# One core, Trainium2: w_in blocks reordered, the SSD groups and GLA heads laid beside the weight stream at fixed pieces

## The reference

```
proj = h @ w_in                      # 256 x 20,560 columns; z, xbc, dt, q, k, v, g, gk, two gates
xbc  = silu(conv4(xbc) + b)          # 4096 columns x, then 1024 B, 1024 C
# SSD: 64 heads in 8 groups, chunks of 128 tokens
seg  = a_cs[i] - a_cs[j];  decay = exp(where(i >= j, seg, -inf))
y    = (C B^T * decay) (x dt) + exp(a_cs) C state_before + D x
y    = grouped_rms_norm(y * silu(z))
# GLA: 4 heads, chunks of 64 tokens
gk   = log_sigmoid(gk_lr @ W + b) / 16;  G = cumsum(gk) in a chunk
o    = tril((q/16 e^G)(k e^-G)^T) v + (q/16 e^G) S
S    = e^{G_last} S + (k e^{G_last - G})^T v
o    = rms_norm(o) * silu(g)
merged = sigmoid(gate_s) * (y @ w_ssd_branch) + sigmoid(gate_g) * (o @ w_gla_branch)
return merged @ w_out
```

## Time and profile before

| what | value |
|---|---|
| time, median of 3 runs | 3322.92 us (3320.24 to 3323.34) |
| time of the profiled execution | 3322.72 us |
| its span | 3321.2 us |
| TensorE matmul busy | 3054.7 us, 92% |
| VectorE busy | 1859.4 us, 56% |
| ScalarE busy | 1442.5 us, 43% |
| GpSimd busy | 57.8 us, 2% |
| mean granted clock of TensorE | 0.957 |

### The profile page before, as it was taken

The page is one execution under the profiler, slowest core; times in us unless marked ns, Lnnn a source line. Parts: engine busy times, 40 slices in busy tenths (PEclk is TensorE's granted clock), DMA queues, the critical chain, the costliest instruction groups (busy, mean ns, idle before and its releaser), DMA issues.

```text
span 3321.2 us, 35212 instructions
## 1 busy us (share of the span) xinstructions
PE 3054.7 (92%) x13922; PEld 2496.4 (75%) x13922; DVE 1859.4 (56%) x2379; ACT 1442.5 (43%) x1865; POOL 57.8 (2%) x37
## 2 busy tenths in 40 slices
PE   9999999899889999799899999999788898888898
PEld 7888887777768666578688888887677677777676
DVE  4444446777675555555555645555545646545645
ACT  4444445444544444444443434434434445434444
POOL 0000000100110000000000000000000000000000
PEclk8999999999999999899999999999899999899899
DMA  6777775555557455476466565655566566666564
GB/s 213 218 220 218 217 227 170 165 184 188 173 168 262 139 184 166 149 265 213 159 194 178 199 190 180 204 174 178 181 191 194 173 201 195 196 198 191 177 188 159
DMA packets 348474, 634.25 MB, mean 191 GB/s; under 512 B 37328, under 2 KB 60180, under 8 KB 345236
## 3 DMA queue, kind: packets, MB, share of 16 engines
q1 hardware_dynamic: 268736, 506.13, 49.6%
q10 hardware_dynamic: 79572, 125.85, 11.2%
HBM read 578.47 MB, written 53.43 MB: 190 GB/s over the span
## 4 chain that ended last, share of the span: by engine, by line
PE 73%; DVE 12%; DMA 6%; ACT 5%; ACTq 2%; issue 2%; DVEq 0%
PE bank L873 21%; PE bank L875 21%; PE bank L874 21%; DVE w_lo L1482 4%; DVE arena L1569 2%; ACT w_hi L903 2%; PE bank L479 2%; DMA arena<-in_sin 1%; PE bank L726 1%; PE bank L745 1%; PE bank L547 1%; ACTq L1346 1%; PE bank L638 1%; PE bank L645 1%; ACT arena L982 1%
## 5 line engine op out<-in xcount | busy, mean ns | idle before, releaser
L1482 DVE TENSOR_TENSOR w_lo<-raw,w_hi 128x1024 fp32r<-128x1024 f32 (+2 forms) x980 | 1174.5, 1217 | 1051.9 <-ACT w_hi L903 1044.0
L873 PE MATMUL bank<-w_lo,x_hi 128*128 128x512 f32 (+1 forms) x3920 | 1555.6, 397 | 28.3 <-DVE stage L1987 19.1
L874 PE MATMUL bank<-w_hi,x_hi 128*128 128x512 f32 (+1 forms) x3920 | 1533.3, 391 | 0.0
L875 PE MATMUL bank<-w_hi,x_lo 128*128 128x512 f32 (+1 forms) x3920 | 1533.2, 391 | 0.0
L903 ACT ACTIVATE w_hi<-raw 128x1024 fp32r<-128x1024 f32 (+2 forms) x980 | 999.0, 1044 | 1097.0 <-PE bank L875 582.5
L873 PEld LDWEIGHTS bank<-w_lo,x_hi 128*128 128x128 f32 x3920 | 750.4, 191 | 194.1 <-DVE stage L1987 20.3
L875 PEld LDWEIGHTS bank<-w_hi,x_lo 128*128 128x128 f32 x3920 | 748.5, 191 | 154.6
L874 PEld LDWEIGHTS bank<-w_hi,x_hi 128*128 128x128 f32 x3920 | 750.3, 191 | 148.7 <-issue 1.9
L908 ACT ACTIVATE x_hi<-bank 128x512 fp32r<-128x512 f32 (+1 forms) x120 | 66.9, 589 | 258.6 <-PE bank L479 253.1
L479 PE MATMUL bank<-ident,arena 128*128 128x128 f32 x472 | 80.7, 330 | 105.9 <-DVE arena L1782 48.2
L1487 DVE TENSOR_TENSOR x_lo<-bank,x_hi 128x512 fp32r<-128x512 f32 (+1 forms) x120 | 78.2, 679 | 164.5 <-ACT x_hi L908 163.9
(11 more groups left out here) (180 smaller groups left out, 1270.8 us busy)
## 6 DMA issues: line engine op xcount, KB each, us to landing
raw<-in_w_in SPq DMA_DIRECT2D x496, 512.0 KB, 4.5
raw<-in_w_up SPq DMA_DIRECT2D x128, 512.0 KB, 3.9
raw<-in_w_down SPq DMA_DIRECT2D x128, 512.0 KB, 4.7
raw<-in_w_out SPq DMA_DIRECT2D x96, 512.0 KB, 4.4
raw<-in_w_ssd_branch SPq DMA_DIRECT2D x64, 512.0 KB, 5.5
proj<-stage ACTq DMA_DIRECT2D x62, 512.0 KB, 6.3
arena<-proj ACTq DMA_DIRECT2D x52, 512.0 KB, 5.3
raw<-in_w_gla_branch SPq DMA_DIRECT2D x32, 512.0 KB, 5.7
```

The source lines that it names most:

```text
L873: pe.matmul(o, x_hi[:, xk, tokens(t)], w_lo[:, r, k, 0:b.n], start=a, stop=False)
L874: pe.matmul(o, x_hi[:, xk, tokens(t)], w_hi[:, r, k, 0:b.n], start=False, stop=False)
L875: op = pe.matmul(o, x_lo[:, xk, tokens(t)], w_hi[:, r, k, 0:b.n], start=False, stop=z_)
L1482: TT(w_lo[:, p % SPLIT_RING, 0:b.per, 0:b.n], raw[:, p % RAW_RING, 0:b.per, 0:b.n], w_hi[:, p % SPLIT_RING, 0:b.per, 0:b.n].bitcast(F32), ...
```

## The change

- `AHEAD` is 6 instead of 4; the ring of 8 stays. `LEAD` (6) takes the place of AHEAD in the start of `latents`; `2 * AHEAD` becomes 8 as before.
- The drain stays at the fourth piece (`DRAIN`), the store is issued at the sixth (`STORE`).
- Side work is started at absolute pieces, and its steps lie at fixed distances from there (`Beside`, `SSD_STEP`, `GLA_STEP`). Groups begin at pieces 54, 80, ..., 236, heads at 268, 294, 320, 346. Several can run at once. The w_in order becomes B and C, then x, z and q/k/v in turn for each group, then g, then the gates.
- The decays: a_cs of all heads is turned once, stored to DRAM (`decays`) and loaded for each group by a broadcast to all partitions (1 MB); ScalarE computes relu(a_cs[i] - a_cs[j]) by 16 Relu and then Exp(-that); VectorE multiplies by C B^T, where GpSimd did.
- Groups 0 to 3 are turned straight into x tiles 16 to 31; groups 4 to 7 go through DRAM and are turned beside the last w_in block (`turned_lower`). w_ssd_branch is read in an order that suits this, and its last block in another, so that `heads_o` can be turned beside it.
- GLA works without passing a state: products between 64-token chunks within a tile of 128 and from tile 0 to tile 1 are made with decayed keys, so a head has one attention matrix and three output products. q and k are turned before they are scaled; the sums come out turned (4 matmuls); a reciprocal becomes Exp(-ln).

```diff
-AHEAD = 4
+AHEAD = 6
+DRAIN, STORE = 3, 5
+LEAD = 6
+SSD_FIRST, SSD_PACE = 54, 26
+GLA_PACE = 26
+SSD_UPPER = 4
+SSD_STEP = {"load": 0, "u": 3, "dec": 6, "bt": 8, "z": 10, "x": 12, "y": 16, "off": 19, "out": 23}
+GLA_STEP = {"gk": 0, "qk": 3, "cs": 8, "att": 13, "o": 17, "out": 20}
...
+    def reach(self, p, every):
+        while self.coming and self.coming[0][0] <= p:
+            at, name, info = self.coming.pop(0)
+            self.running.append([at, at, self.stages[name](*info)])
+        for one in list(self.running):
+            while one[1] <= p:
+                after = next(one[2], "over")
+                if after == "over":
+                    self.running.remove(one)
+                    break
+                one[1] = p + every if after is None else one[0] + after
...
     for g in range(SSD_G):
-        into(COL_GATE + g * BLK, ("ssd", g))
-        into(COL_Q + (g + 1) * BLK).ends = True
+        into(COL_XBC + g * BLK)
+        into(COL_Z + g * BLK)
+        into(COL_Q + g * BLK)
+    for j in range((COL_GK - COL_G) // BLK):
+        into(COL_G + j * BLK)
+    for j in range(2 * NB):
+        into(COL_GATE + j * BLK)
+    for g in range(SSD_G):
+        sides.append((SSD_FIRST + g * SSD_PACE, "ssd", (g,)))
+    at = SSD_FIRST + SSD_G * SSD_PACE
+    sides.append((at, "gla_begin", ()))
+    for h in range(GLA_H):
+        sides.append((at + 6 + h * GLA_PACE, "gla", (h,)))
+    beside(blocks[-1], "lower", at=0)
...
         def ssd_group(g):
-            pe.wait_ge(*ssd.dve["gt", g])
-            for (t, hb), b in DEC_BANK.items():
-                for h in range(HB):
-                    op = pe.matmul(bank[b][:, h * P:(h + 1) * P],
-                                   wide(gt[:, AA + t, hb * HB + h:hb * HB + h + 1], [P, P]), tri,
-                                   start=True, stop=True)
...
+            act.dma_start(dec.rearrange("p t h n -> p t (h n)"),
+                          bass.AP(decays.tensor, g * SSD_HG * P, [[0, P], [SSD_H * P, NT], [1, SSD_HG * P]])).then_inc(
+                *load[2]("ssd", g))
...
+            for t, hb in DEC_PARTS:
+                for h in range(hb * HB, (hb + 1) * HB):
+                    op = A(dec[:, t, h, :], dec[:, t, h, :], ACT.Relu, bias=gt[:, CS + t, h:h + 1], scale=-1.0)
+                op.then_inc(*ssd.act("lag", g, t, hb))
...
+            yield GLA_STEP["o"]
+            pe.wait_ge(*gla.dve["att", h])
+            pe.wait_ge(*gla.act["cross", h])
+            for t in range(NT):
+                op = pe.matmul(bank[5 + t][:, :], att[:, t, :], g_v[:, t, :], start=True, stop=(t == 0))
+                if t:
+                    op = pe.matmul(bank[6][:, :], att[:, NT, :], g_v[:, 0, :], start=False, stop=True)
+                op.then_inc(*gla.pe("o", h, t))
```

More of the change, by code:

```diff
@@ L35 @@
 COL_XBC = SSD_IN
+COL_BC = COL_XBC + SSD_IN
 COL_DT = COL_XBC + SSD_IN + 2 * SSD_G * SSD_N
@@ L191, in schedule @@
         if j == 0:
-            b.before, b.side = [("heads_o",)], ("sum_begins", 0)
+            beside(b, "sum_begins", 0)
     b.ends = True
@@ L243, in schedule @@
             if j == 0:
-                b.side = ("neighbour", l)
+                beside(b, "neighbour", l)
         b.ends = True
@@ L700, in latents @@
         def latents(l):
-            for _ in range(AHEAD):
+            for _ in range(LEAD):
                 yield
@@ L710, in latents @@
                 yield
-            for _ in range(2 * AHEAD):
+            for _ in range(8):
                 yield
@@ L936, in ssd_shared @@
         def ssd_shared():
-            for _ in range(AHEAD):
-                yield
+            yield 6
             act.wait_ge(*stored[0][0])
@@ new lines, in turn_heads_o @@
+        def turn_heads_o():
+            act.wait_ge(*side_out["heads_o", GLA_H - 1])
+            act.wait_ge(*gla.dve["out", GLA_H - 1])
+            act.wait_ge(*gla.pe["o", GLA_H - 1, NT - 1])
+            for n in range(NB):
+                act.dma_start(total[:, :, n * BLK:(n + 1) * BLK], heads_o[:, :, n * BLK:(n + 1) * BLK]).then_inc(
+                    *load[n]("heads_o", n))
+            begin = start_of["ssd_branch", NB - 1].first
+            for n in range(NB):
+                for t in range(NT):
+                    k = 2 * n + t
+                    yield 3 + 3 * n + t
+                    act.wait_ge(*merge.pe["o_turned", k])
+                    act.wait_ge(*summed[begin + 2 * n + 1])
+                    high(4 + k % 4, 4 * n, t).then_inc(*merge.act("o_hi", k))
@@ L2101, in sync @@
             col = 0
-            for part in b.weight(q):
+            for part in b.weight(b.order[q]):
                 width = part.shape[-1]
```

823 lines of the change are left out of this document (405 added, 418 removed).

## The result

The changed kernel took 3148.32 us (median of 4 runs, 3145.47 to 3149.9) beside 3323.13 us for the kernel before: ratio 0.9473, 95% interval 0.9456 to 0.9489. The forecast was 3150 us. The profiled execution has a span of 3148.2 us.

A forecast was written before the change was run, and what follows sets the result against it. TensorE, busy nearly always, was taken as the bound, with waits and slow clock beside SSD and GLA. Span 3321.2 less 209.3 in the first stretch plus 37 given back is 3148.9, time 3150 us; range 3100 to 3215.

The forecast's parts named there:

- TensorE's own work, end at 1183.5, and 10 us of waits, 1193.5: First stretch: 689.5 us of TensorE work after 494.0, plus waits of 3 us (group 0) and 7 us (11 groups and heads).
- A group takes 79 us, VectorE 58 of it, ScalarE 48: SSD group of 26 pieces: 71 us stream plus 8 side work; VectorE 58, ScalarE 48, or some 54 with DMA issues.
- The walk through a group: SSD group timed from T, the end of piece 3: side results ready before TensorE asks, smallest margin 3 us.
- The Relus: 0.26 us each: ScalarE in each SSD group: 16 new Relus of 128x128 at 0.26 us each, 4.2 us.
- Rival A: First stretch: ring absorbs less than walked; 1.5 us lost per handoff, about 70 us, time 3215; chance 0.18.
- C: SSD groups: the 1 MB broadcast load of decays lands far later; at 45 us the time is 3342; chance 0.04.
- B: Outside the first stretch: AHEAD 6 costs nothing elsewhere, time 3113; chance 0.15 for this and below.
- D: First stretch: fixed places collide and most waits return elsewhere, 145 us back, time 3295; chance 0.06.
- What AHEAD gives back: Later stages: AHEAD 6 starts side work up to 5.44 us later; 37 us given back, bounds 0 and 60.
- `gla_branch`: Its drains with gates: margin 3.8 us, short by 1.6, four times, 6 us given back.
- `neighbour`: Attention layers: its 20 load issues and kt copies move by 5.4 us, so TensorE waits 5.4 more a layer.
- The short latent blocks: Attention layers: 21 us of waits in place of 13, 8 more a layer, bounds -5 and +12.

The follow-up runs named there:

- the runs at steps 9 and 10: Changed kernel with TensorE's transposes of x asked for at step 9 or 10 of a group in place of 12: 3209.7 us and 3172.1 us.
- as the run shows: Changed kernel with the 16 Relus of ScalarE replaced by 16 subtract-and-min operations of VectorE: 3151.9 us, ratio 0.948.

## Why the prediction was right

Point by point, by its own steps:

- **TensorE's own work, end at 1183.5, and 10 us of waits, 1193.5.** Measured 1191.8, the start of the first w_gla_branch piece. (The forecast calls this point the end of the last `ssd_branch` piece; in the kernel before the two lay 20.8 us apart, the serial turn of `heads_o` between them.) Idle in the whole first stretch were 3.3 us, so the 7 us allowed for eleven groups and heads were hardly used and the 3 for group 0 not at all, and TensorE's own work was some 5 us more than counted. These two errors cancel to 1.7 us. The work has two errors of its own: counted in the trace from the start of each matmul to the next, idle time left out, the bursts are 93.6 us and not 102, and the stream's matmuls are 14 more than forecast. Why a piece of the stream beside bursts takes a little over 2.72 us wasn't looked into. (The sum also takes the tail off twice in the turns on the spot: four times 0.9 is 3.6, not 3.2.) The decays' share is shown by putting them back (28.4 us in the stretch, 28 forecast).
- **A group takes 79 us, VectorE 58 of it, ScalarE 48.** The loads of the decays are issued from 163.7 to 718.2, seven groups apart: 79.2 us each. VectorE was busy 375.20 us in that window, 53.6 a group and 4.4 less than forecast, ScalarE 349.15, 49.9 (its issues, which the 54 of the forecast has too, don't count as busy). Of VectorE's 4.4 some 3 are time that it lost beside GpSimd in the kernel before (last section): the forecast carried it over as VectorE's own work.

```profile
163.70:718.20 554.50, 554.50 (x2638) 460.70 (x2637) 375.20 (x520) 349.15 (x535) 0.00 (x0) 1.00 0.69 229
```

- **The walk through a group.** With T at 649.62, where TensorE turns u in group 4: ScalarE's timeline has the last four SiLUs end at 672.84, T + 23.2 (forecast T + 23), and TensorE turns x at 676.04, T + 26.4 (T + 26).

```profile
671.14 1.31 ACT L1015 ACTIVATE arena<-arena 128x256 f32<-128x256 f32 x3
...
672.35 0.49 ACT L1015 ACTIVATE arena<-arena 128x256 f32<-128x256 f32 x1
```

  The earlier points come out as well: the Exps end at T + 18.3 (T + 18), the products of the decays at T + 24.6 (T + 24). The 3.2 us between the last SiLU and the turn are the smallest margin of the walk; the runs at steps 9 and 10 used it up and paid 5.1 and 2.4 us a group, as it says.
- **The Relus: 0.26 us each was too little.** One lasts 0.388 us in the trace and 16 take 4.78, 0.30 each, where the sum had 4.2. The estimate by the Trainium skill (ScalarE: Activation LUTs, What ACT_TABLE_LOAD costs), 0.39 us for one before overlap, agrees with the 0.388. The rule of the Trainium skill in the same page's Rules for kernel authors, relu on VectorE, holds here for the busy time (3.23 us against 4.78) and not for the time of this kernel, as the run shows.
- **Rival A, 1.5 us a handoff:** idle time of 3.3 us in the stretch excludes it. **C** is excluded by the landings, 12.2 us at most, **B** by the layers' 36.4 us and by the run with depth 4 alone, **D** by the length of the first stretch.
- **What AHEAD gives back: 37 forecast, 38 measured, with errors in it that cancel.** `gla_branch`: four waits of 1.6 forecast; four came, 5.5 us in all, but the kernel before had already paid one of 3.0 there, which I had not taken off, and the stage grew by 1.9 and not 6. The latents: 2 us more a layer forecast, 2.6 measured. `neighbour`: 5.4 more a layer forecast, and here the step itself is wrong: the wait of the kt product is 3.2 us a layer and not 8.4. The waits for the loads, for the kt product and for the turned probabilities (L747, L756 and L775, 17.5 us; before 13.8) grew by 1.9 a layer: the new one is for the loads, 3.5, one step ahead of the kt product, and that for the probabilities shrank by 1.8. The short latent blocks: 8 more a layer forecast, 5.9 measured; the wait ahead of ukv0 is 13.8 and not 16. Not in the sum at all: the heads' queries and keys (L1899), 2.9 a layer. By the run with AHEAD 4 alone these stay (35.7 us), and with LEAD 4 and the earlier stores they go (27.0), so they come from the start or store of the latents, not from the depth. The kernel before with depth and start changed, and the store not, has 34.9, which speaks for the start. The short blocks' wait is in the larger part of the same kind: 26.0 us of the 30.9 stay with AHEAD 4 alone, 14.8 with LEAD 4 and the earlier stores.
- **The slow clock behind waits: the term that was missing.** All these waits make 27.4 us for both layers, where 31 were forecast; the layers took 36.4. The other 9.0 are the same matmuls at a lower granted clock: in the layers TensorE was busy 69.3 us while the granted clock was 0.50, and 48.9 in the kernel before; half of the difference is 10. The prediction priced each new wait at its own length. The run at step 9 shows some 7 us for a wait of 5.
- **"Granted clock 1.00 throughout the first stretch"** holds from 37.4 us on. The 0.98 of the first row is the start alone: 0.50 from 13.7 to 37.4, as in the kernel before from 14.4 to 38.7 (0.51).

The gain itself is 91.8 us of idle time and 118.5 of busy time. Of the busy time 28 are the decays. The kept traces divide the rest. These two groups of the kernel before, the state updates and the carried products of the GLA heads, are gone:

```profile
L638 PE MATMUL bank<-arena 64*128 64x512 f32 x48 | 23.8, 615 | 0.0
L645 PE MATMUL bank<-arena 128*64 128x512 f32 x48 | 23.2, 605 | 0.0
```

Counted from start to start they are 45 us, and all bursts together (those at granted clock 0.50 counted half) fell from 172 us, where the prediction had 175, to 93.6: 78 less, the decays among them. And from 494.0 to 1402.8 TensorE had been busy 72.8 us while the granted clock was 0.50; in the changed kernel there is none of that between 37.4 and 1191.8. If such matmuls take twice as long, that is 36 us; at the rate of the run at step 9, where 39.4 us of them cost 16.9, it is 31. Both are estimates. So of the 211 us some 92 are waits, 31 to 36 the clock behind them, 78 work that is no longer done, and 5 to 10 stay unassigned.

## What to carry to other kernels

When one engine's stream is the bound, put each handoff of the side work at the piece where the walk says that its input is ready, with a few us to spare: here 3 us were enough, a longer stretch for the GLA heads was not needed, and two pieces too early cost 24 us. A deeper run-ahead of a ring is not free: everything that the same engine does beside the ring starts that much later, so measure it by itself; here it cost 28 us in the layers and bought nothing, and taking it back gave the best version. Price a wait of TensorE at more than its length: here some 40% more at 5 us. And if another engine's work goes away, look whether it had slowed the engines that stay before carrying their busy time over.

## What the hardware showed that was not expected

- A wait of 4.8 to 5.3 us of TensorE, in the midst of dense work, was followed eight times out of eight by some 4 us of work at granted clock 0.50 (2.9 to 6.1), which made it about 7 us; waits of 2.1 to 2.6 us were followed by it twice out of eight.
- VectorE's rows were slower while POOL worked. In the kernel before, two sets of the convolution's later taps in group 4; POOL multiplies from 781.95 to 789.17, beside the second:

```profile
779.01 2.46 DVE L1569 SCALAR_TENSOR_TENSOR arena<-arena 128x256 f32<-128x256 f32 x6
...
786.54 4.50 DVE L1569 SCALAR_TENSOR_TENSOR arena<-arena 128x256 f32<-128x256 f32 x6
```

  Of the 144 such operations 15 lay beside POOL's for more than half of their time, and they had a mean of 1485 ns, the other 129 one of 477; of VectorE's splits in the SSD stretch 16 had 1831 ns beside POOL, the rest 1221. In the changed kernel, with POOL's multiplications gone, the 144 take 59.1 us in place of 74.2 (L1638, mean 480 ns). Together that is some 25 us, 3 a group. Why the engines compete isn't shown.
